# Retention heads normed, gated and split one by one, with the output projection waiting for each quarter's chunks

## What is computed

```
def retention_mixer(h, positions, w_in, gn_g, w_out):
    q, k, v, g = jnp.split(h @ w_in, [hk, 2 * hk, 2 * hk + hv], axis=-1)
    ...
    _, o = lax.scan(step, state0, (to_blocks(q, RET_CHUNK), to_blocks(k, RET_CHUNK), to_blocks(v, RET_CHUNK)))
    o = from_blocks(o)
    o = o * lax.rsqrt(jnp.mean(o * o, axis=-1, keepdims=True) + EPS)
    o = o.reshape(b, s, hv) * gn_g.astype(jnp.float32)
    o = (jax.nn.silu(g.astype(jnp.float32)) * o).astype(h.dtype)
    return o @ w_out
```

## Time and profile before

| | us |
|---|---|
| median of three runs | 3152.53 |
| the three runs | 3151.2, 3152.53, 3154.91 |
| the profiled execution, its own time | 3147.0 |
| its span | 3144.9 |
| mean granted clock of TensorE | 0.958 |
| TensorE busy | 2762.9 (88%) |
| VectorE busy | 1166.2 (37%) |
| ScalarE busy | 940.1 (30%) |
| DMA | 796.04 MB, 253 GB/s on average |

### The profile page before, as it was taken

How to read it: one execution, slowest core, us unless ns; L and a number is a source line. 1 busy time by engine, 2 the same in 40 slices (tenths; PEclk the granted TensorE clock), 3 DMA queues, 4 the chain that set the end, 5 groups by cost and what they waited for, 6 DMA issues and landing times.

```text
span 3144.9 us, 35285 instructions
## 1 busy us (share of the span) xinstructions
PE 2762.9 (88%) x13676; PEld 1736.4 (55%) x13676; DVE 1166.2 (37%) x2116; ACT 940.1 (30%) x1712; POOL 45.8 (1%) x51
## 2 busy tenths in 40 slices
PE   7999877777888887777789999898999979989898
PEld 3444322222553442222255788857879968875787
DVE  1662200011332320000135544547666355443766
ACT  2113201101212320000024443545444445433543
POOL 0020000000000000000000000000000000000000
PEclk9999999999999999999998999999999999998999
DMA  7573599999521849999950666582555415662152
GB/s 326 244 316 136 239 427 429 428 429 428 232 80 70 330 195 427 429 428 429 428 242 1 273 267 255 204 331 89 190 198 191 157 57 241 280 266 99 54 187 93
DMA packets 59486, 796.04 MB, mean 253 GB/s; under 512 B 8636, under 2 KB 9916, under 8 KB 10748
## 3 DMA queue, kind: packets, MB, share of 16 engines
q1 hardware_dynamic: 55664, 790.13, 61.4%
q10 hardware_dynamic: 3724, 4.59, 0.4%
HBM read 793.64 MB, written 1.05 MB: 253 GB/s over the span
## 4 chain that ended last, share of the span: by engine, by line
PE 68%; DMA 21%; DVE 5%; ACT 3%; issue 2%; SPq 0%; ACTq 0%; DVEq 0%; POOL 0%; POOLq 0%
DMA ring<-in_t_up 20%; PE banks L1845 11%; PE banks L1421 8%; PE banks L762 6%; PE banks L894 5%; PE banks L1833 5%; PE banks L909 4%; PE banks L1296 4%; PE banks L1826 4%; PE banks L744 3%; PE banks L1829 2%; PE banks L1542 1%; PE banks L1024 1%; PE banks L1306 1%; PE banks L663 1%
## 5 line engine op out<-in xcount | busy, mean ns | idle before, releaser
L1421 PE MATMUL banks<-ring,arena 128*64 128x512 f32 x2048 | 480.1, 623 | 123.0 <-DMA ring<-in_t_up 67.5
L2749 DVE TENSOR_TENSOR ring_lo<-ring,w_hi 128x1024 fp32r<-128x1024 f32 x256 | 312.5, 1225 | 289.0 <-ACT w_hi L2178 288.6
L1421 PEld LDWEIGHTS banks<-ring,arena 128*64 128x64 f32 x2048 | 166.4, 143 | 435.0 <-issue 388.0
L2178 ACT CAST w_hi<-ring 128x1024 fp32r<-128x1024 f32 x256 | 267.9, 1053 | 402.3 <-PE banks L1845 199.0
L2372 DVE TENSOR_TENSOR arena<-arena,banks 128x512 f32<-128x512 f32 x32 | 22.0, 687 | 815.9 <-PE banks L1421 815.9
L1437 PE MATMUL banks<-ring,arena 128*64 128x512 f32 x1024 | 236.8, 617 | 33.9 <-DMA ring<-in_t_down 22.6
L1943 ACT COPY arena<-banks 32x512 f32 x96 | 55.3, 576 | 616.3 <-PE banks L1437 615.6
L1845 PE MATMUL banks<-w_hi,ffn_h_hi 128*128 128x512 f32 x512 | 202.0, 395 | 0.0
L762 PE MATMUL banks<-arena,ring 128*128 128x512 f32 (+1 forms) x512 | 185.3, 524 | 16.9 <-ACT arena L703 16.9
L1845 PE MATMUL banks<-w_hi,ffn_h_lo 128*128 128x512 f32 x512 | 199.6, 390 | 0.0
L1845 PE MATMUL banks<-ring_lo,ffn_h_hi 128*128 128x512 f32 x512 | 199.5, 390 | 0.0
(11 more groups left out here) (353 smaller groups left out, 4024.8 us busy)
## 6 DMA issues: line engine op xcount, KB each, us to landing
ring<-in_t_ada SPq DMA_DIRECT2D x72, 2048.0 KB, 9.1
ring<-in_t_gate SPq DMA_DIRECT2D x64, 2048.0 KB, 17.1
ring<-in_t_up SPq DMA_DIRECT2D x64, 2048.0 KB, 17.3
ring<-in_t_down SPq DMA_DIRECT2D x64, 2048.0 KB, 17.2
ring<-in_t_ffn SPq DMA_DIRECT2D x64, 2048.0 KB, 12.0
ring<-in_t_ret_in SPq DMA_DIRECT2D x12, 2048.0 KB, 7.8
ring<-in_t_in_cd SPq DMA_DIRECT2D x6, 2048.0 KB, 18.9
ring<-in_t_sb_in SPq DMA_DIRECT2D x6, 2048.0 KB, 13.3
```

What stands on the lines that cost most here:

```text
L1421: mm = nc.tensor.matmul(PS[64 * h:64 * h + 64, f.bank, :], x_cur[:, b, k, :], wview(un[h0 + h], KC)[:, k, :], start=(k == 0), stop=(k == K ...
L2178: nc.scalar.copy(w_hi[:, n % 4], w).then_inc(S("ffn_w_hi"), 1)
L2749: TT(w_lo, w, w_hi[:, n % 4].bitcast(F32), ALU.subtract).then_inc(S("ffn_w_lo"), 1)
```

## The change

In words:

- *Banks.* A value product pair (two chunks of a head) now shares one bank: `pv` has 8 results instead of 16.
- *No copy.* ScalarE squares 512 columns straight from the bank into `rt_sq`, which has a second pair of buffers for odd heads. VectorE norms straight from the bank, one chunk at a time, then gates and makes low parts by pairs.
- *Order by head.* TensorE's queue takes value pairs and the sums of heads in turn, and quarters 0 and 1 ahead of the value pairs of head 3. ScalarE and VectorE do norm, gate, high and low part for each head, with the weight quarters 0 to 7 set in between. `rt_o_hi` of a head lies over the values `rt_v` of that head.
- *Waits.* Quarter n below 8 waits for `rt_o_lo` to reach n + 1, instead of quarter 0 for all 16.
- *Gains.* `gp_pe` moves ahead of quarters 5 and 12, and `gp_dve` behind the low parts of quarters 9 and 13.
- *Slots.* The output projection's weight slots are the two halves of `hT_r` and a third at the place of `rt_decay`. `rt_rs` keeps two heads.

The diff, cut to its core:

```diff
-        rt_out_slots = [region_r("rt_out_w", W + 14848, [KC, P])] + half_slots
+        rt_out_slots = half_slots + [region_r("rt_out_w", W, [KC, P])]
...
-                fills(p + "pv", [0, 1, 2, 3] * 4)
+                fills(p + "pv", [0, 1, 2, 3, 4, 5, 2, 3])
...
-        rt_rs = region(W + 13824, [4, N])
+        rt_rs = region(W + 1024, [2, N])
...
-        rt_o_hi = region_r("rt_o_hi", W + 9728, [16, N])
+        rt_o_hi = region_r("rt_o_hi", W + 9728, [2, 4, 2, N])
+        rt_sq = [[SQ[:, 0, :], SQ[:, 1, :]], [region(W + 15360, [512]), region(W + 15872 + 512, [512])]]
...
+                values(0, 0)
+                values(0, 1)
+                values(1, 0)
+                head_ms(0)
+                values(1, 1)
+                values(2, 0)
+                head_ms(1)
+                values(2, 1)
+                head_ms(2)
+
+                def before_quarter(n):
+
+                    if n == 2:
+                        values(3, 0)
+                        values(3, 1)
+                    if n == 3:
+                        head_ms(3)
+                    if n == 5:
+                        gp_pe(pe, i, 0)
+                    if n == 12:
+                        gp_pe(pe, i, 1)
+                    if n < 8:
+                        pe.wait_ge(S("rt_o_lo"), n + 1)
...
-                for m, f in enumerate(plan[p + "pv"]):
-                    copy_act(act, f, rt_o[:, m, :], PS[:, f.bank, 0:N])
-                for h in range(4):
-                    stat_act(act, c, [(rt_o[:, 4 * h + q, :], plan[p + "pv"][4 * h + q].free) for q in range(4)],
-                             plan[p + "ms"][h], N)
-                    rsqrt_act(act, c, plan[p + "ms"][h], N, 512, dst=rt_rs[:, h, :])
...
+                def head_sq(h, n):
+
+                    f = plan[p + "pv"][2 * h + n]
+                    f.full.wait(act)
+                    if h >= 2:
+                        plan[p + "ms"][h - 2].full.wait(act)
+                    nc.scalar.activation(rt_sq[h % 2][n], PS[:, f.bank, :], ACT.Square).then_inc(S("rt_sq"), 1)
...
+                weight(0)
+                weight(1)
+                plan[p + "s"][3].free.wait(act)
+                weight(2)
+                head_sq(0, 0)
+                head_sq(0, 1)
+                head_sq(1, 0)
+                head_root(0)
+                head_sq(1, 1)
+                head_sq(2, 0)
+                head_hi(0)
+                head_root(1)
+                head_sq(2, 1)
+                head_root(2)
+                head_hi(1)
+                weight(3)
+                weight(4)
+                head_sq(3, 0)
+                head_sq(3, 1)
+                head_hi(2)
+                weight(5)
+                head_root(3)
+                weight(6)
+                head_hi(3)
+                weight(7)
...
+                for n in range(3):
+                    lo_dve(dve, qs[n])
+                head_norm(0)
+                head_gate(0)
+                head_lo(0)
+                head_norm(1)
+                head_gate(1)
+                head_lo(1)
+                lo_dve(dve, qs[3])
+                head_norm(2)
+                head_gate(2)
+                lo_dve(dve, qs[4])
+                head_lo(2)
+                lo_dve(dve, qs[5])
+                head_norm(3)
+                head_gate(3)
+                lo_dve(dve, qs[6])
+                head_lo(3)
+                lo_dve(dve, qs[7])
...
+                gp_at = (9, 13) if kind == "ret" else (1, 4)
```

More of the change, by code:

```diff
@@ L1786, in ret_pe, with values @@
                     f.free.wait(pe)
-                for h in range(4):
+                def values(h, n):
+                    f = plan[p + "pv"][2 * h + n]
                     plan[p + "s"][h].free.wait(pe)
[L1789 to L1801, removed]
+                    f.open(pe)
+                    for q in range(2):
+                        e = slice(h * 512 + (2 * n + q) * P, h * 512 + (2 * n + q + 1) * P)
+                        nc.tensor.matmul(PS[:, f.bank, q * N:(q + 1) * N], rt_v[:, 0, e], rt_s[:, h, 0:N],
+                                         start=True, stop=False)
+                        mm = nc.tensor.matmul(PS[:, f.bank, q * N + P:(q + 1) * N], rt_v[:, 1, e], rt_s[:, h, N:384],
+                                              start=False, stop=True)
@@ new lines, in values, with head_ms @@
+                    mm.then_inc(f.full.sem, 1)
+                def head_ms(h):
+                    f = plan[p + "ms"][h]
+                    f.open(pe)
+                    for n in range(2):
+                        pe.wait_ge(S("rt_sq"), 2 * h + n + 1)
+                        for q in range(2):
+                            mm = nc.tensor.matmul(PS[:, f.bank, 0:N], ones[:, :], rt_sq[h % 2][n][:, q * N:(q + 1) * N],
+                                                  start=(n == 0 and q == 0), stop=(n == 1 and q == 1))
+                    mm.then_inc(f.full.sem, 1)
@@ L1803, in ffn_pe @@
+                split_pe(pe, p + "out", hi=lambda q: rt_o_hi[:, q % 4 // 2, q // 4, q % 2, :],
+                         lo=lambda q: rt_o_lo[:, q, :], between={n: lambda n=n: before_quarter(n) for n in range(16)})
             def ffn_pe(i):
@@ new lines, in weight @@
+                def weight(n):
+                    if qs[n].before is not None:
+                        qs[n].before.used.wait(act)
+                    hi_act(act, qs[n])
+                def head_sq(h, n):
+                    f = plan[p + "pv"][2 * h + n]
+                    f.full.wait(act)
+                    if h >= 2:
+                        plan[p + "ms"][h - 2].full.wait(act)
+                    nc.scalar.activation(rt_sq[h % 2][n], PS[:, f.bank, :], ACT.Square).then_inc(S("rt_sq"), 1)
@@ new lines, in head_root, with head_hi @@
+                def head_root(h):
+                    if h >= 2:
+                        plan[p + "pv"][2 * h - 3].free.wait(act)
+                    rsqrt_act(act, c, plan[p + "ms"][h], N, 512, dst=rt_rs[:, h % 2, :])
+                def head_hi(h):
+                    for n in range(2):
+                        act.wait_ge(S("rt_o"), 2 * h + n + 1)
+                        nc.scalar.copy(rt_o_hi[:, n, h, :, :], rt_o[:, 4 * h + 2 * n:4 * h + 2 * n + 2, :])\
+                            .then_inc(S("rt_o_hi"), 1)
@@ L2799, in closed @@
                         post_dve(dve, c, i, 0, name)
-                split_dve(dve, [p + "out"], closed,
-                          between={1: lambda: gp_dve(dve, i, 0), 4: lambda: gp_dve(dve, i, 1)})
+                gp_at = (9, 13) if kind == "ret" else (1, 4)
+                split_dve(dve, [p + "out"], closed, first=8 if kind == "ret" else 0,
+                          between={at: lambda which=which: gp_dve(dve, i, which) for which, at in enumerate(gp_at)})
                 ffn_lo(i, 0, 0)
```

35 lines of the change are left out of this document (21 added, 14 removed).

## The result

The changed kernel took 3134.18 us in the median of 5 runs (3131.98 to 3140.53) against 3152.53 for the kernel before (5 runs, 3146.52 to 3154.91): a ratio of 0.9947, 95% interval 0.9935 to 0.9959. Timed twice more, beside other kernels, it gave 3131.17 (ratio 0.9939, 0.9925 to 0.9953) and 3132.64 (0.9941, 0.9928 to 0.9955). The prediction was 3133.2, range 3128 to 3139.

The account below looks back on a forecast made before the run. TensorE was taken as the bound, waiting in the retention stage on a serial norm, gate, split, weight chain. 64.5 us of work plus 0.6 unknown gives 65.1 instead of 84.4, 19.3 less: 3152.5 to 3133.2 us, range 3128 to 3139.

Parts of the forecast that it names:

- The same forecast for a profiled execution: Whole kernel: the profiled execution of 3147.0 us, by its own time, moves to 3127.7 us.
- Work that stays: TensorE in the retention stage: value chunks 10.5, sums 7.0, gain products 3.5, quarters 43.5, together 64.5 us.
- Removed waits: Retention stage: gaps around the sums 7.6, wait before quarter 0 9.5, slow first quarter 2.5, together 19.6 us.
- What covers the waits: Retention stage, three queues followed: every product finds its inputs at least 2 us early once quarter 0 has begun.
- The unknown: Retention stage: hand-overs cost 0.1 to 1.5 us, switching from fp32 products nothing to 0.6; 0.6 us taken in all.
- Edits at no cost: Retention stage: norm read from banks, fewer gate and part instructions, third weight slot, second square buffer, moved gains cost nothing.
- the tight places: Ahead of quarter 0: sums of head 0, 1 and 2 come 0.4, 0.4 and 0.0 us after their last square.
- the 19.3 us are kept: Behind the stage: later stretches move as they are, no TensorE wait for DMA found, so the 19.3 us stay.
- rival B, the clock elsewhere: Outside the stage: slow clock stretches shift, 2.5 us either way, 3130.5 to 3136 us; chance 0.13.
- A (hand-overs, 3 to 6 us): Stage's first 13 us: queues catch on one another, 3 to 6 us lost, 3136 to 3139 us; chance 0.12.
- C (waiting for all heads): Output projection: quarter 0 in fact waits for all four heads, 3147 to 3150 us; chance 0.03.
- D (half clock through the quarters): Stage: clock falls to 1.2 GHz in the fp32 part and through all quarters, 3174 us; chance 0.02.

Follow-up runs that it names:

- before_warm: Kernel before, with 40 bf16 products of zeros that nobody reads filling TensorE's idle 9.5 us ahead of quarter 0; 3148.56 us, ratio 0.9993.
- chain of runs: Changed kernel, then with all four heads ahead of quarter 0, then also with one wait for all low parts; 3134.18, 3138.33 and 3143.26 us.
- wait_all: Changed kernel with all four heads ahead of quarter 0 and quarter 0 waiting for the low parts of all heads; 3143.26 us, ratio 0.9977.
- before_weights_first: Kernel before, with the first three weight quarters split ahead of the value chunks and a wait per quarter; 3145.74 us, ratio 0.9986.
- loaded kernel: Three changed kernels with added copies ahead of the squares, squares made twice, or scaled products made twice; 3132.91, 3137.45 and 3135.91 us.
- squares_twice: Changed kernel with each square of heads 0 to 2 made twice on ScalarE; 3137.45 us, one run.
- gains_in_pause: Changed kernel with the second gain product, in all four blocks, moved from the output projection into the pause behind it; 3122.90 us, ratio 0.9912.
- pauses_warm: As gains_in_pause, with TensorE's pauses ahead of the transposes filled with bf16 products of zeros that nobody reads; 3108.52 us, ratio 0.9868 against the kernel before.
- heads_first: Changed kernel with all four heads ahead of quarter 0 on the three queues, wait per quarter kept; 3138.33 us, ratio 0.9962.
- after_again: Changed kernel with no edit, timed and profiled a second time; 3131.17 us, ratio 0.9939 against the kernel before.

## Why the prediction was right

The mechanism was right: the waits of the stage are gone, and it takes 64.73 us where 65.1 were forecast. That the time, 3134.18 us, came within 1 us of the 3133.2 is in part luck: the stage gave 0.4 us more than forecast, not all of it reached the time, and the sum started from a median, 3152.53, that lies above the 3150.0 of all 50 runs of the kernel before. The same forecast for a profiled execution, 3127.7 us, missed: the three took 3134.2 to 3136.2.

**Work that stays, 64.5 us.** Right. The stage took 64.73 with all of it in one piece; the sums 7.0 and the quarters 2.72 each are confirmed by it.

**Removed waits, 19.6 us.** Right, and their parts too. The clock's 2.5 us measured 2.6 in `before_warm`. The whole splits along the chain of runs, into 7.7 us for heads one by one and all else that `wait_all` has of the change, 8.4 for the wait per quarter on top of that (with the clock's share) and 3.55 for head 3 behind quarter 1, together 19.7. The split depends on the order in which the parts are added: on the kernel before, first weights and the wait per quarter without the heads gave 6.9 (`before_weights_first`). The 84.4 come from a single profile of the kernel before; `before_warm` repeats its start of quarter 0, origin + 36.31, to a hundredth.

**What covers the waits.** Followed queue by queue, this gave quarter 2 at 21.2 us behind the origin, quarter 4 at 28.3, quarter 6 at 35.4. Measured from 2513.40: 21.15, 28.45 and 35.71. Rows of VectorE and ScalarE in the changed kernel show how early the inputs are:

```profile
2528.26 1.29 DVE L2840 TENSOR_TENSOR rt_o_lo<-arena,rt_o_hi 128x512 fp32r<-128x512 f32 x2 [0.81 <-ACT rt_o_hi L2226]
```

```profile
2522.51 1.22 ACT L2226 CAST rt_o_hi<-arena 128x512 fp32r<-128x512 f32 x2
```

Head 1's low parts end at 2529.55 and quarter 2 starts at 2534.55, 5 us later; a high part of 512 columns takes about 0.6 us, as estimated. Where the prediction named the tight places, the sums of head 0 to 2, it was right: every loaded kernel broke at head 2's. What it didn't say is that VectorE's load arrives there too.

**The unknown.** 0.6 us were taken for hand-overs and switching together, 0.23 were there (64.73 - 64.5). Nothing of it is a wait that the view shows. Switching does show: the first product of quarter 0 costs 0.42 us to the next start and that of quarter 2 costs 0.32, where the others cost 0.23. The ends 0.1 and 2.1 held.

**Edits at no cost.** The norm read from the banks was booked as free, and it is cheap cover rather than a gain: its undoing costs 0.47 us. By form, VectorE's scaled products out of the banks took this long (count, busy us, mean ns, idle before):

```profile
L2822 DVE SCALAR_TENSOR_TENSOR arena<-banks,V,arena 128x256 f32<-128x256 f32 x16 | 6.6, 477 | 3.2 <-ACT arena L679 3.1
```

That is 477 ns against 479 for the same operation out of SBUF. The Trainium skill, "VectorE: DVE Perf Modes", section on the TRN2 errata, gives a PSUM source 62 cycles more of fixed time; the trace does not agree, and the prediction went by the row.

**Behind the stage: "the 19.3 us are kept".** This step did not hold in full. In the three comparisons of the changed kernel the medians differ by 18.4, 18.8 and 17.9 us. Over all 50 runs of the kernel before (median 3150.0) and 15 of the changed one (3132.8) it is 17.3, where the stage alone gives 19.7. The other kernels point the same way. Leaving out `squares_twice`, which has one run, and `gains_in_pause` and `pauses_warm`, which change other places too, each gained less against the kernel before than its stage did, by 1.0 us (`wait_all`) to 4.5 (`heads_first`). The profiles show where it can go. The whole part behind the stage took 552.4 us in the kernel before, 552.5 and 554.0 in the two others built from it, and 553.6 to 556.9 in the eight profiles built from the changed one without moving the gains. From the transposes ahead of block 3 to that block's first gain product the kernel before took 93.85 us, the changed one 94.29, 97.08 and 94.28. In after_again the clock stays low longer, beside a TensorE that is busy (first the changed kernel's first profile, then the second):

```profile
2882.00:2892.00 10.00, 9.94 (x43) 0.96 0.01 2
```

```profile
2882.00:2892.00 10.00, 9.97 (x33) 0.66 0.01 2
```

This is rival B, the clock elsewhere, which had 2.5 us either way in the prediction. Its mechanism was right and its size too small for a single execution: behind the stage it cost up to 4.5 us, and ahead of it, where the change can't reach, the origin moved over 6.05 us, from 2507.86 to 2513.91, among kernels that are alike there. Its effect on the median stays inside the range. That all kernels fall short the same way speaks against chance alone, but why a stage that ends earlier should meet a lower clock behind it is not shown. Nor is it shown that the stage of the kernel before, profiled once, takes 84.4 us in every execution: its slow first quarter hangs on the clock too.

**Rivals A, C and D.** A (hand-overs, 3 to 6 us) did not happen, and the loaded kernels show how far off it was: even with 3 us of squares more TensorE lost half a microsecond. C (waiting for all heads) was made on purpose in `wait_all`: a stage of 76.7 and 3143 us, less than the 3147 to 3150 given: that price put the last low parts at 32.1 us behind the origin (2540.2), where the changed order has them, and with head 3 pulled ahead on all engines they were there at 27.6. D (half clock through the quarters) has no trace: clock 1.00 in every stretch of the stage.

## What to carry to other kernels

Read the wait that ends last in a stage and ask how much of what it waits for the first product needs; then put the first weights and the first parts ahead of it on every engine, and let the later parts arrive behind products that already run. An order like this can be costed before it is built by following each engine's queue with durations from the trace: here it was right to 0.4 us in 65 for the stage, while 1 to 2.4 us less than the stage gave reached the time. Once a stage is full, move out of it what a pause can hold, and look at the clock behind each pause: filling the pauses, even with products that nobody reads, was worth 14 us here, against 18 for the original change.

## What the runs showed of the hardware

TensorE's granted clock fell to 0.50 (1.2 GHz) in or behind gaps of 9 us, of 4.4 and 7.9 us and also of 3.44 us, and in the last case only 1.2 us after work had resumed. The length of a gap did not decide alone: behind the four gaps of 2.58 us in `gains_in_pause` it fell twice and stayed at 1.00 twice. Filling the gap with bf16 products of zeros kept it at 1.00 (2.4 GHz) each time: that gave 2.6 us behind the heads, and at each of the transposes 1.4 to 2.6 us against the profiles of the changed kernel (with the gain products moved in four of the eight places). The Trainium skill, "TensorE: Matmul & The Clock Gate", Part 1, says that "the default state is throttled, and activity releases the throttle"; the filled gaps agree. The ten microseconds at 0.66 with TensorE busy 9.97 of 10.00, above, don't follow from that sentence, and why they stay low was not tried.

How long the clock stays low differs from one execution to the next: the same instructions reached the same product 6 us apart, and 15 runs of the changed kernel lay within 10.4 us (3130.1 to 3140.5). A difference of a few microseconds is better read from the stage in the profile, which repeated to 0.01 us in the changed kernel, than from medians.
